# Expert weight blocks: sixteen places used in turn and two used once, in place of twelve in turn and seven used once

## The reference

```
x = layer_norm(DEEPNORM_ALPHA * x + (1 + gt_m) * y, ln_g[l, 0], ln_b[l, 0])
h = x * (1 + sc_f) + sh_f
y = hier_moe(h, ...)      # 32 experts of width 512 in 4 groups, 2 experts a token
x = layer_norm(DEEPNORM_ALPHA * x + (1 + gt_f) * y, ln_g[l, 1], ln_b[l, 1])
```

## Time and profile before

| | us |
|---|---|
| median of 3 runs | 2504.77 (2504.33 to 2505.61) |
| the profiled execution's own time | 2500.56 |
| its span | 2498.8 |
| TensorE (PE) busy | 2351.4 (94%) |
| VectorE (DVE) busy | 1259.5 (50%) |
| ScalarE (ACT) busy | 746.8 (30%) |
| gpsimd (POOL) busy | 200.0 (8%) |
| moved by DMA | 689.71 MB, mean 276 GB/s |

### The profile page before, as it was taken

The page is one execution under the profiler, slowest core; times in us unless marked ns, Lnnn a source line. Parts: engine busy times, 40 slices in busy tenths (PEclk is TensorE's granted clock), DMA queues, the critical chain, the costliest instruction groups (busy, mean ns, idle before and its releaser), DMA issues.

```text
span 2498.8 us, 39961 instructions
## 1 busy us (share of the span) xinstructions
PE 2351.4 (94%) x15930; PEld 1596.2 (64%) x15930; DVE 1259.5 (50%) x1902; ACT 746.8 (30%) x1113; POOL 200.0 (8%) x308
## 2 busy tenths in 40 slices
PE   8999999999999999999999999899889999999896
PEld 7997689978997799744884443333357644333332
DVE  7864678757876685553564322222177543222213
ACT  4334653344335633312211111111035521111111
POOL 1100201000100210020240000000000300000000
PEclk9999999999999999999999999999999999999998
DMA  8865458755873485453007899999965399999996
GB/s 343 304 257 170 150 204 322 267 202 196 310 269 135 149 298 183 136 180 115 17 4 264 348 420 422 422 422 422 421 260 185 126 380 371 421 422 422 422 422 261
DMA packets 108994, 689.71 MB, mean 276 GB/s; under 512 B 14812, under 2 KB 16156, under 8 KB 33992
## 3 DMA queue, kind: packets, MB, share of 16 engines
q1 hardware_dynamic: 88720, 618.10, 63.1%
q0 software_dynamic: 20096, 69.81, 7.7%
q10 hardware_dynamic: 56, 0.06, 0.0%
HBM read 686.82 MB, written 1.11 MB: 275 GB/s over the span
## 4 chain that ended last, share of the span: by engine, by line
PE 69%; DMA 20%; DVE 5%; ACT 2%; issue 2%; SPq 0%; POOL 0%; DVEq 0%; ACTq 0%
PE bank L844 67%; DMA ring<-in_moe_wup 10%; DMA B<-in_moe_wgate 9%; PE bank L842 2%; DMA ring<-in_moe_wdown 1%; ACT B L1831 1%; DVE ring_r L2260 1%; DVE xt_r L2241 0%; ACT B_r L1770 0%; ACT B L1890 0%; DVE B L2764 0%; DMA ring<-in_ffn_w_gate 0%; DVE B L2954 0%; DVE small_s L2645 0%; DVE X L2643 0%
## 5 line engine op out<-in xcount | busy, mean ns | idle before, releaser
L2260 DVE TENSOR_TENSOR ring_r<-ring,B_r 128x2048 fp32r<-128x2048 f32 x181 | 410.7, 2288 | 228.7 <-ACT B_r L1770 228.2
L844 PE MATMUL bank<-B_r 128*128 128x512 f32 (+1 forms) x1892 | 489.2, 347 | 8.6 <-DVE B_r L2618 6.0
L844 PE MATMUL bank<-ring,B 128*64 128x512 f32 (+1 forms) x1712 | 438.7, 600 | 24.6 <-DMA ring<-in_moe_wup 14.4
L1770 ACT ACTIVATE B_r<-ring 128x2048 fp32r<-128x2048 f32 x184 | 347.3, 1911 | 266.0 <-PE bank L844 263.5
L844 PE MATMUL bank<-xt_r,B_r 128*128 128x256 f32 x1408 | 393.7, 280 | 4.3 <-DVE ring_r L2260 2.4
L844 PE MATMUL bank<-xt_r,ring_r 128*128 128x256 f32 x1408 | 394.5, 281 | 0.0
L844 PEld LDWEIGHTS bank<-B_r 128*128 128x128 f32 x1892 | 321.0, 189 | 100.8 <-issue 47.1
L844 PEld LDWEIGHTS bank<-ring,B 128*64 128x64 f32 (+1 forms) x1712 | 152.4, 144 | 274.2 <-issue 256.0
L844 PEld LDWEIGHTS bank<-xt_r,B_r 128*128 128x128 f32 x1408 | 266.1, 189 | 8.2 <-issue 6.6
L844 PEld LDWEIGHTS bank<-xt_r,ring_r 128*128 128x128 f32 x1408 | 265.4, 188 | 0.0
L844 PE MATMUL bank<-rows,B 128*64 128x512 f32 x480 | 215.5, 594 | 42.7 <-DMA lo_mix<-in_moe_wgate 26.3
(11 more groups left out here) (378 smaller groups left out, 2914.4 us busy)
## 6 DMA issues: line engine op xcount, KB each, us to landing
ring<-in_moe_wdown SPq DMA_DIRECT2D x114, 1024.0 KB, 22.8
ring<-in_moe_wup SPq DMA_DIRECT2D x62, 1024.0 KB, 23.6
rows<-in_moe_wgate SPq DMA_DIRECT2D x56, 1024.0 KB, 23.4
wks<-in_moe_wup SPq DMA_DIRECT2D x56, 1024.0 KB, 22.9
ring<-in_ffn_w_gate SPq DMA_DIRECT2D x44, 1024.0 KB, 4.9
ring<-in_ffn_w_up SPq DMA_DIRECT2D x44, 1024.0 KB, 7.9
ring<-in_ffn_w_down SPq DMA_DIRECT2D x44, 1024.0 KB, 7.7
wks<-in_ada_w POOLq DMA_DIRECT2D x72, 512.0 KB, 6.4
```

Of the source, the lines that this page charges most:

```text
L844: ins = pe.matmul(out, lhsT, rhs, start=start, stop=stop, skip_group_check=True)
L1770: act.activation(hi, ring[:, slot, :], ACT.Copy).then_inc(sp_hi, 1)
L2260: dve.tensor_tensor(ring_r[:, slot, :], ring[:, slot, :], f32(hi), ALU.subtract).then_inc(sp_lo, 1)
```

## The change

ONCE shrinks to units 7 and 11 (B7 and B1). MORE grows to ten: the two `spare` tiles, `xt` and the piece of B4 and B5 join the places used in turn, so there are sixteen of these. X is no place any more, so it isn't restored from its halves, nothing waits for the halves, and gain and bias are applied to X ahead of the first pair. `take_expert` fixes the ring's position when a layer of experts begins. The loop on SP has 3 rounds of 48 units, and the last 24 are written out. The `spare` loads for layer 1 wait for all releases of layer 0. `EXPERT_UNITS` (units that release a place) goes from 185 to 190, and with it the unit after which `ln_b1` and `ln_b3` may be loaded. Some semaphores are merged (`once_landed`, `fx_pe` into `lg_pe`, `xm_act` into `lo_act`, one increment less of `mo_hi`).

```diff
@@ -24,8 +24,8 @@
 NSLAB = DFF // SLAB
 LAYERS = 2
 R = 6
-MORE, MORE_AT = 6, 5
-ONCE = (7, 11, 20, 21, 22, 19, 18)
+MORE, MORE_AT = 10, 5
+ONCE = (7, 11)
 UNIT = 2048
 BANK = 512
 NEG = -1.0e30
...
@@ -130,18 +131,21 @@
     def begin_experts(self):
-        self.turn = 0
+        self.turn, self.base = 0, self.pos
     def take_expert(self):
         at = self.turn % (R + MORE)
         self.turn += 1
-        return self._at(R + at - MORE_AT if MORE_AT <= at < MORE_AT + MORE else self.pos % R, 1)
+        if MORE_AT <= at < MORE_AT + MORE:
+            return self._at(R + at - MORE_AT, 1)
+        return self._at((self.base + min(at, MORE_AT)) % R, 1)
     def skip_second_trunk(self):
         for dmas in [3] + [1] * 14 + [2] + [1] * 4:
             self.take(dmas)
+        self.begin_experts()
         for _ in range(EXPERT_UNITS):
             self.take_expert()
...
@@ -349,13 +353,10 @@
         more = [rows[:, 0:2, :].rearrange("p a b -> p (a b)"), B[8][:].rearrange("p a b -> p (a b)"),
                 rows[:, 2:4, :].rearrange("p a b -> p (a b)"), lo_mix[:], wks[:, 0:UNIT], wks[:, UNIT:2 * UNIT]]
-        once = [B[7][:].rearrange("p a b -> p (a b)"), B[1][:].rearrange("p a b -> p (a b)"),
-                nc.alloc_sbuf_tensor_at("B4_B5", [P, UNIT], F32, offset=place["B4"] + 4 * D)[:]] + \
-               [spare[:, i, :] for i in range(2)] + [xt[:].rearrange("p k t -> p (k t)"), X[:].rearrange("p a b -> p (a b)")]
-
-        def landed_at(x):
-
-            return max(x - 1, 0) if x < 3 else 2
+        more += [spare[:, i, :] for i in range(2)] + [
+            xt[:].rearrange("p k t -> p (k t)"),
+            nc.alloc_sbuf_tensor_at("B4_B5", [P, UNIT], F32, offset=place["B4"] + 4 * D)[:]]
+        once = [B[7][:].rearrange("p a b -> p (a b)"), B[1][:].rearrange("p a b -> p (a b)")]
         def panel(slot):
             return ring[:, slot, :] if slot < R else more[slot - R]
...
@@ -705,13 +704,25 @@
             def ffn_n(n):
                 ffn(*[A[f"ffn{1 + n % 2}_w_{x}"][n // 2] for x in ("gate", "up", "down")])
+            def expert_source(l, i, n):
+
+                return A[("moe_wgate_2", "moe_wup_2", "moe_wdown_2")[n // 4]][l]\
+                    .rearrange("(i e) (p u k) n -> i e u p (k n)", e=2, u=2, p=P)[i, n % 2, n % 4 // 2]
+
+            opening = [n for n in range(24) if n not in ONCE]
+
+            def open_slot(l, t):
+
+                slot = R + t - MORE_AT
+                i, n = divmod(opening[t], 12)
+                sp.dma_start(panel(slot), expert_source(l, i, n)).then_inc(w_landed[slot], 16)
+
             def open_spare(l):
-                for x in (3, 4):
-                    i, n = divmod(ONCE[x], 12)
-                    w = A[("moe_wgate_2", "moe_wup_2", "moe_wdown_2")[n // 4]][l]
-                    sp.dma_start(once[x], w.rearrange("(i e) (p u k) n -> i e u p (k n)", e=2, u=2, p=P)
-                                 [i, n % 2, n % 4 // 2]).then_inc(once_landed[2], 16)
+                if l:
+                    sp.wait_ge(w_free, MOE_AT[0] + EXPERT_UNITS + R)
+                for x in (6, 7):
+                    open_slot(l, MORE_AT + x)
             def finish():
                 for h in range(TB):
...
@@ -752,58 +763,50 @@
                     sp.wait_ge(w_free, pos - MORE)
                     sp.dma_start(panel(slot), source(i, n)).then_inc(w_landed[slot], 16)
-                opening = [n for n in range(24) if n not in ONCE]
                 cur.begin_experts()
                 place_of = [cur.take_expert() for _ in range(R + MORE)]
-                def open_slot(t):
-
-                    slot, _, _ = place_of[t]
+                def open_ring(t):
+
+                    slot, _, pos = place_of[t]
+                    sp.wait_ge(w_free, pos if t < MORE_AT else pos - MORE)
                     i, n = divmod(opening[t], 12)
                     sp.dma_start(panel(slot), source(i, n)).then_inc(w_landed[slot], 16)
-                def open_ring(t):
-
-                    pos = place_of[t][2]
-                    sp.wait_ge(w_free, pos if t < MORE_AT else pos - MORE)
-                    open_slot(t)
-
                 def open_once(x):
                     i, n = divmod(ONCE[x], 12)
-                    sp.dma_start(once[x], source(i, n)).then_inc(once_landed[landed_at(x)], 16)
+                    sp.dma_start(once[x], source(i, n)).then_inc(once_landed, 16)
                 for t in (0, 1):
                     open_ring(t)
                 if l == 0:
                     sp.wait_ge(tr_src, TRANS_AT["y_r"] + 1)
-                    for t in range(MORE_AT, MORE_AT + MORE):
-                        open_slot(t)
+                    for x in (0, 1, 2, 3, 4, 5, 9):
+                        open_slot(l, MORE_AT + x)
                     open_once(0)
-                    open_once(2)
                 else:
                     sp.wait_ge(at_lo, H // 2 * 3)
-                    for x in (0, 1, 2, 4):
-                        open_slot(MORE_AT + x)
-                    open_once(2)
+                    for x in (0, 1, 2, 4, 9):
+                        open_slot(l, MORE_AT + x)
                 for t in (2, 3, 4, MORE_AT + MORE):
                     open_ring(t)
                 if l:
                     sp.wait_ge(pj_pe, PROJ_DONE[PROJ_AT["wo_f"] + 1] + TB)
                     for x in (3, 5):
-                        open_slot(MORE_AT + x)
+                        open_slot(l, MORE_AT + x)
                     open_once(0)
                 sp.wait_ge(tr_src, TRANS_AT[f"moe{l}"] + 1)
                 open_once(1)
                 sp.wait_ge(rt_pe, 2 * l + 1)
-                open_once(5)
-                sp.wait_ge(mo_hi, 3 * l + 3)
-                open_once(6)
+                open_slot(l, MORE_AT + 8)
                 for n in opening[R + MORE:]:
                     load_next(1, n - 12)
-                with cur.loop(sp, PAIRS - 2, R + MORE, R + MORE) as i:
-                    for n in range(12):
-                        load_next(i + 2, n)
+                with cur.loop(sp, PAIRS // 4 - 1, 48, R + MORE) as i:
+                    for n in range(48):
+                        load_next(i * 4 + (2 + n // 12), n % 12)
+                for n in range(24):
+                    load_next(PAIRS - 2 + n // 12, n % 12)
                 w = [x.rearrange("i e u p q -> (i e) p u q") for x in (g, u, d)]
                 with overflowed(sp, l):
...
@@ -1173,9 +1176,8 @@
             def expert_unit(opening, n):
                 if opening and n in ONCE:
-                    x = ONCE.index(n)
-                    pe.wait_ge(once_landed[landed_at(x)], (32, 32, 16, 64)[min(x, 3)] * opening)
-                    return once[x]
+                    pe.wait_ge(once_landed, 16 * len(ONCE) * opening)
+                    return once[ONCE.index(n)]
                 slot, landed, _ = cur.take_expert()
                 pe.wait_ge(w_landed[slot], landed)
                 return panel(slot)
...
@@ -2544,10 +2546,9 @@
             def moe(l):
                 dve.tensor_copy(Xhi[:, 0, :, :], by_chunk(0)).then_inc(mo_hi, 1)
                 transposes(f"moe{l}", xt)
-                dve.wait_ge(mo_hi, 3 * l + 2)
+                dve.wait_ge(mo_hi, 2 * l + 2)
                 for t in range(TB):
-                    ins = dve.tensor_tensor(Xlo[:, t, :, :], by_chunk(t), f32(Xhi[:, t, :, :]), ALU.subtract)
-                ins.then_inc(mo_hi, 1)
+                    dve.tensor_tensor(Xlo[:, t, :, :], by_chunk(t), f32(Xhi[:, t, :, :]), ALU.subtract)
                 route(l)
                 def pack(e0):
...
@@ -2625,12 +2626,9 @@
                 n = PAIRS * l
                 for c in (1, 3):
                     packed(XeT[0], c, bank[4 + c], 2 * n + c + 1)
-                quad(n, 4, first=True)
-                for t in range(TB):
-                    ins = dve.tensor_tensor(by_chunk(t), f32(Xhi[:, t, :, :]), f32(Xlo[:, t, :, :]), ALU.add)
-                link(ins)
                 norm_gain(2 * l)
                 norm_bias(2 * l)
+                quad(n, 4, first=True)
                 with dve.Fori(0, PAIRS // 4 - 1) as i:
                     quad(n + 2, i * 8 + 8, i)
                     quad(n + 4, i * 8 + 12, i)
```

More of the change, by code:

```diff
@@ L118, in __init__ @@
         self.pos, self.lots, self.i, self.per, self.span, self.turn = 0, [0] * (R + MORE), None, 0, R, 0
+        self.base = 0
     def _at(self, slot, dmas):
@@ L466, in build @@
         w_landed = [sem(f"w_landed{i}") for i in range(R + MORE)]
-        once_landed = [sem(f"once_landed{i}") for i in range(3)]
+        once_landed = sem("once_landed")
         w_free = sem("w_free")
@@ L572, in build @@
         fx_act = sem("fx_act")
-        fx_pe = sem("fx_pe")
         fx_aug = sem("fx_aug")
@@ L578, in build @@
         col_set = sem("col_set")
-        xm_act = sem("xm_act")
         fx_dve = sem("fx_dve")
@@ L1645, in _ @@
                        signal=pj_pe if k == KC - 1 else None)
-            pe.wait_ge(xm_act, 1)
```

(9 more changed lines are left out.)

## The result

The changed kernel takes 2486.39 us (median of 6 runs, 2483.37 to 2490.81), the kernel before in the same comparison 2504.49 us (6 runs, 2496.44 to 2505.61). The ratio is 0.9937, 95% interval 0.9924 to 0.995: 12.5 to 19 us faster. Run again beside other kernels it gave 0.9948 (0.9929 to 0.9968). I had said 2494.3, range 2490 to 2500.

A forecast was written before the change was run, and what follows sets the result against it. It took the expert stages as bound by the DMA refill stream, 2.486 us a block plus standstills. Terms -6.8 - 6.3 - 1.8 + 5.0 - 0.6 = -10.5 us took 2504.8 to 2494.3 us, range 2490 to 2500.

The forecast's parts named there:

- Holes closed: DMA standstills at 1414 to 1426 (layer 0) and 2070 to 2078 (layer 1) vanish: -6.8 and -6.3 us.
- small holes: Idle DMA at 1390 to 1398 and 2042 to 2050, covered by gpsimd's earlier row broadcasts: -1.8 us together.
- theory A: Follow-up experiments' count: until unit 23 is released, the stream carries only as many blocks as places released; 10.5 us a layer idle.
- One block fewer at the start: Eighteen blocks instead of nineteen have a place when TensorE starts; +2.486 us in each layer, +5.0 us.
- VectorE at no price: X's restoring removed, gain and bias moved ahead of the first pair into VectorE's free time: 0 us.
- Row for the next norm: gpsimd's ln_b1 and ln_b3 broadcasts issue later; in layer 1 behind the last awaited landing: -0.6 us; layer 0: 0.
- R1: Layer 0's gain is lost in the trunk between the layers, only layer 1 counts: -5.3, 2499.5 us; 8%.
- R2: The new places are slower to write, or the longer queue costs 1% of the stream: 8.7 us return, 2503 us; 6%.
- R3: SP, not lack of places, holds the stream; the hole stays and the missing block costs +5.0: 2509.8 us; 4%.
- R4: SP's loop body grows from 12 to 48 issues and its returns stall the stream: 2515 us at 28 us each; 2%.

The follow-up runs named there:

- spread: Kernel before with the seven once-used units at 7, 11, 13, 16, 18, 20, 22 instead of 7, 11 and 18 to 22; ratio 1.0001 to the kernel before.
- twelve_two: Changed kernel without the four new places: twelve in turn, two used once, fourteen blocks at the start; ratio 1.0008 to the kernel before.
- no_x_place: Kernel before with X's tile no longer a place (twelve in turn, six used once), X still restored late; ratio 1.0004 to the kernel before.
- norm_late: Changed kernel with the norm's gain and bias back behind the first two pairs; ratio 0.9955 to the kernel before.
- row_late: Kernel before with the row broadcasts for ln_b1 and ln_b3 waiting for three more releases; ratio 0.9994 to the kernel before.

## Why the prediction was right in kind and wrong in size

**What failed is the term "Holes closed", with the small holes beside it.** They were sized as 12 x (1 - 0.44/1.01) = 6.8 and 6.3 us, together 13.1, and 1.8 for the small ones: 14.9 us, with 2.4 more allowed for if the early broadcasts fitted into the idle stretch ahead. 19.2 us came back. Two things made the term too small. The first is the share: the same rows give bytes, and where the queue is thin they say less than the share. In the earlier trace rows the line 1390 to 1398 has 0.89 of share but 328 of 422 GB/s: 8 x (1 - 328/422) = 1.8 us lost, not 0.95. The line 1414 to 1426 has 162 GB/s: 7.4 us, not 6.8. The second is the windows, which cut the holes short, in layer 1 above all. These rows are set by the router's first maximum of each execution. They show 14 to 82 us behind it (layer 0, then layer 1), first of the kernel before, then of the changed one, and then, for the kernel before, the small and the large hole of each layer:

```profile
1371.51:1439.51 68.00, 67.74 (x360) 28.93 (x357) 22.95 (x29) 10.47 (x23) 1.06 (x2) 1.00 0.85 337
2024.89:2092.89 68.00, 67.73 (x362) 29.30 (x359) 22.96 (x29) 11.17 (x24) 1.06 (x2) 1.00 0.86 342
```

```profile
1368.87:1436.87 68.00, 67.74 (x358) 28.73 (x355) 17.87 (x26) 10.26 (x23) 1.06 (x2) 1.00 0.96 396
2018.71:2086.71 68.00, 67.74 (x362) 29.29 (x359) 16.97 (x26) 11.15 (x24) 1.06 (x2) 1.00 0.98 402
```

```profile
1389.51:1405.51 16.00, 16.00 (x74) 5.93 (x72) 3.31 (x6) 1.68 (x3) 0.00 (x0) 1.00 0.95 366
1413.51:1429.51 16.00, 15.87 (x84) 6.16 (x83) 7.57 (x8) 3.06 (x8) 0.00 (x0) 1.00 0.58 220
2042.89:2058.89 16.00, 16.00 (x76) 5.98 (x74) 3.77 (x6) 1.68 (x3) 0.00 (x0) 1.00 0.92 358
2066.89:2082.89 16.00, 15.87 (x81) 6.04 (x80) 8.04 (x8) 2.70 (x6) 0.00 (x0) 1.00 0.60 227
```

The kernel before loses 13.7 and 12.9 us, the changed one 4.2 and 3.2: 9.5 and 9.7 us less. The large holes are worth 7.7 and 7.4 us and not 6.8 and 6.3, the small ones 2.1 and 2.4 and not 0.95 and 0.87. With 2.5 for the block more, the stream wins 7.0 and 7.2 us a layer; the prediction had 5.3 and 4.7. The count of theory A needs no windows and has 10.5 - 2.5 = 8.0, about 1 us too much a layer.

**The reason given for the hole was wrong too.** The prediction said that five once-units in a row make it. In spread they don't follow each other, and the stream is idle as long as before. What makes it is that seven of the first 24 units release nothing.

**Point by point.**
- *One block fewer at the start, +5.0.* Right where the stream is full, as in the changed kernel (twelve_two: four blocks more, 18.0 us). Wrong as a price in itself: while the stream starves, a place used once gives a block at the start and takes a release away, and the two cancel (no_x_place, 1.7 us for two layers instead of 5.0, of which about 1 is clock).
- *Small holes, covered by the broadcasts.* Right in kind: full at 417 GB/s after, open again in norm_late. gpsimd issued them at 1370.48 and 1372.63, as forecast.
- *VectorE at no price.* Gain and bias ran at 1367.58 and 1369.97, inside the free stretch, and TensorE stayed busy.
- *Row for the next norm, -0.6.* It was worth nothing (row_late against spread: 19.2 us in both). The last wait behind it grew by what the earlier one lost.
- *R1.* The trunk grew by 3.5 us in the profiled execution, but by a fall of TensorE's clock; again it was 182.1 against 181.3 us. Layer 0's part arrived.
- *R2.* SP issues into xt at 1545.97 and at 1784.54 with 96 blocks from the one to the other: 2.485 us a block, against 2.486 before. No place is slower.
- *R3 and R4.* The holes closed, and the written-out loop is no faster. The rule that stood beside R4 (the Trainium skill, Runtime: NRT & Kernel Launch, section Instruction fetch mechanics) may hold; no run here shows such a fetch, and whatever it takes doesn't show in the stages.

The two timeline rows behind R2, issues into xt in the changed kernel:

```profile
1545.97 2.00 SPq L764 DMA_DIRECT2D xt<-in_moe_wdown  x1
...
1784.54 2.13 SPq L764 DMA_DIRECT2D xt<-in_moe_wdown  x1
```

Summed up: -7.0 and -7.2 us for the stream and nothing for the row make -14.2 us. The stages say -15.9, of which 1.6 are the clock in layer 1 of the kernel before, so -14.3. The second execution says -13.9; without that 1.6, and without the 0.7 us that its own clock costs at the end of layer 1, that is -13.0. From 2504.5 us the stream's -14.2 would lead to 2490.3, just inside the range; the measured 2486.4 lies 4 us lower, within the interval of the comparison (-12.5 to -19 us). So that the time fell outside the range is in part scatter. That the term "Holes closed" was 4.3 us too small doesn't hang on it.

## What to carry to other kernels

Where a consumer starts on a stock and is fed slower than it eats, count releases: over any opening stretch the feeding stream loses about (time the consumer takes) minus (places released in it) x (time of one transfer). A buffer used once adds to the stock and takes a release away, so it is worth a transfer only if the stream has enough releases without it; here sixteen in turn and two once beat twelve in turn and seven once with one buffer less. Read what a transfer queue loses from bytes per second against the full rate, and check it by such a count. Set the windows of two executions by the same event in each: the openings here lie up to 11 us apart in absolute time, and a window of 4 us at a stream's start then compares different moments.

## What the runs showed of the hardware that I had not expected

- A DMA share near full doesn't mean full rate: 0.89 of share went with 328, 322 and 330 GB/s of 422 in three kernels.
- TensorE's granted clock fell to 0.50 for some 6 us in the trunk of one execution (the row of 8 us shows 0.57), after TensorE had been busy without a break (15.00 of 15 us), and went back to 1.00 with TensorE as busy. In the second execution of the same kernel the trunk is 2.7 us shorter. The trunk with the fall took 2.7 to 3.5 us longer than the others of these two kernels, as much as some of the terms above.
- Such falls also come near the end of a stage that waits for DMA, and there they can pass for the effect of a change: 1.6 us in layer 1 of the kernel before (0.72 from 2470 to 2476). The kernel before spans 2490.42 to 2508.84 us over 28 runs on one chip, while the stages of it and its three near variants (spread, no_x_place, row_late) lie between 470.8 and 474.0 us.
